# Second half's sums behind the first consumer matmuls, chunk masks built inside the first MLP, and a new order of ScalarE's work at the four norm boundaries

## The reference

```
for layer in range(2):
    a = rms_norm(h, norm_gains[layer, 0])
    m = mla_mixer(a, ...) if layer == 0 else hgrn2_mixer(a, ...)
    h = h + rms_norm(m, norm_gains[layer, 1])
    a = rms_norm(h, norm_gains[layer, 2])
    h = h + rms_norm(sq_relu_mlp(a, mlp_w1[layer], mlp_w2[layer]), norm_gains[layer, 3])
```

## Time and profile before

| | |
|---|---|
| runs shown | 1892.26, 1892.64, 1893.92 us; median 1892.64 us |
| profiled execution | 1893.63 us, span of its instructions 1891.7 us |
| mean granted TensorE clock | 0.947 |
| TensorE busy | 1697.2 us, 90% of the span |
| VectorE, ScalarE, GpSimd busy | 45%, 38%, 34% |
| HBM traffic | 73 GB/s over the span |

### The profile page before, as it was taken

One profiled execution on the slowest core, in us unless ns is written; L12 is line 12 of the kernel. 1 busy time (PEld: TensorE's weight loads), 2 busy tenths in 40 slices (PEclk: granted clock), 3 DMA queues, 4 the chain that ended last, 5 costly groups with the idle time before them and its releaser, 6 DMA issues.

```text
span 1891.7 us, 29823 instructions
## 1 busy us (share of the span) xinstructions
PE 1697.2 (90%) x10588; PEld 1374.1 (73%) x10588; DVE 853.8 (45%) x1467; ACT 716.4 (38%) x1129; POOL 635.0 (34%) x385
## 2 busy tenths in 40 slices
PE   4999968768678999899999997899998899999996
PEld 4778727755455676787888887788786787888885
DVE  4634377655566444352212124667664452212124
ACT  1332333322344443461323234666663452323231
POOL 4344500002331112444444445323232453444441
PEclk8999969998888999999999998899999999999997
DMA  9423200001211112323333332222221323333331
GB/s 313 133 78 92 75 11 3 4 2 48 55 37 29 34 36 61 90 68 94 95 90 99 99 93 75 56 56 74 59 78 34 89 78 89 94 95 100 89 100 56
DMA packets 250853, 140.10 MB, mean 74 GB/s; under 512 B 10089, under 2 KB 242624, under 8 KB 250768
## 3 DMA queue, kind: packets, MB, share of 16 engines
q1 hardware_dynamic: 249072, 135.03, 24.7%
q10 hardware_dynamic: 688, 2.23, 0.3%
q0 software_dynamic: 1008, 1.66, 0.3%
HBM read 136.80 MB, written 2.10 MB: 73 GB/s over the span
## 4 chain that ended last, share of the span: by engine, by line
issue 56%; POOL 15%; PE 15%; DVE 7%; DVEq 4%; ACT 1%; POOLq 1%; DMA 1%; ACTq 0%; SPq 0%
POOL w_low L510 13%; PE bank L661 6%; PE bank L805 2%; PE bank L916 2%; DVE bank L1770 1%; DVEq L1777 1%; DVEq L2139 1%; PE bank L819 1%; DVE mix_out L1770 1%; PE bank L1021 0%; DMA w_raw<-in_mlp_w 0%; POOL param_rows L491 0%; DVE kk_norm L1770 0%; DVEq L2075 0%; PE bank L788 0%
## 5 line engine op out<-in xcount | busy, mean ns | idle before, releaser
L510 POOL TENSOR_TENSOR w_low<-w_raw,w_high 128x1024 fp32r<-128x1024 f32 (+1 forms) x232 | 513.7, 2215 | 1124.9 <-ACT w_high L1293 1124.9
L661 PE MATMUL bank<-act_high,w_high 128*128 128x512 f32 x992 | 395.7, 399 | 13.9 <-POOL w_low L510 13.8
L661 PE MATMUL bank<-act_high,w_low 128*128 128x512 f32 x992 | 388.6, 392 | 0.0
L661 PE MATMUL bank<-act_low,w_high 128*128 128x512 f32 x992 | 388.3, 391 | 0.0
L1293 ACT ACTIVATE w_high<-w_raw 128x1024 fp32r<-128x1024 f32 (+1 forms) x232 | 225.2, 971 | 299.7 <-PE bank L661 273.9
L661 PEld LDWEIGHTS bank<-act_high,w_high 128*128 128x128 f32 x992 | 187.3, 189 | 61.1 <-issue 10.2
L661 PEld LDWEIGHTS bank<-act_high,w_low 128*128 128x128 f32 x992 | 187.0, 189 | 40.6
L661 PEld LDWEIGHTS bank<-act_low,w_high 128*128 128x128 f32 x992 | 187.5, 189 | 39.5 <-issue 2.0
L661 PE MATMUL bank<-hid_high,w_high 128*128 128x512 f32 x488 | 192.0, 394 | 3.9 <-DVE mix_out L2357 3.8
L661 PE MATMUL bank<-hid_low,w_high 128*128 128x512 f32 x488 | 191.3, 392 | 0.0
L661 PE MATMUL bank<-hid_high,w_low 128*128 128x512 f32 x488 | 191.0, 391 | 0.0
(11 more groups left out here) (509 smaller groups left out, 2893.4 us busy)
## 6 DMA issues: line engine op xcount, KB each, us to landing
w_raw<-in_mlp_w SPq DMA_DIRECT2D x128, 512.0 KB, 4.0
w_raw<-in_hgrn_w_in SPq DMA_DIRECT2D x32, 512.0 KB, 4.1
w_raw<-in_w_in SPq DMA_DIRECT2D x29, 512.0 KB, 3.9
w_ada_piece<-in_w_ada SPq DMA_DIRECT2D x6, 2048.0 KB, 13.5
w_raw<-in_w_out SPq DMA_DIRECT2D x8, 512.0 KB, 3.8
w_raw<-in_mla_w_o SPq DMA_DIRECT2D x8, 512.0 KB, 3.7
w_raw<-in_hgrn_w_o SPq DMA_DIRECT2D x8, 512.0 KB, 3.7
w_raw<-in_mla_w_in SPq DMA_DIRECT2D x6, 512.0 KB, 3.9
```

What stands on the lines that cost most here:

```text
L510: gp.tensor_tensor(WL[:, c0 % 2, 0:kt, 0:m], WR[:, c0 % 2, 0:kt, 0:m], WH[:, c0 % 2, 0:kt, 0:m].bitcast(F32), ALU.subtract).then_inc(w_lo, 1)
L661: mm = pe.matmul(PB[s][0:m, :], w[:, s, k, 0:m], a[:, k0 + k, :], start=(k == 0 and w is WH and a is hi), stop=(k == kt - 1 and w is WL))
```

## The change

`token_sum(b, 1)` leaves the last producer job. It and `token_stat(b, 1)` now hang on passes 0 and 3 of consumer job 1, and `token_spread(b, 1)` on pass 6 of job 0's `act_low` matmuls. At boundary 3 `token_sum` comes after four transposed tiles. GpSimd builds the chunk masks in four pieces between the splits F0+4 to F0+7 of the first MLP. On ScalarE, `high(c0+5)` and `high_x(c0+6)` go ahead of the square of tile 3, a one-element root is put ahead of the last square of half 0, and `high_x(c0+9)` behind that square.

```
-                             hooks={2: lambda: token_stat(b, 0, n_act)} if k == WHOLE else
-                             {6: lambda: token_sum(b, 1)} if k == KT - 1 else None).then_inc(job_done, 1)
+                             hooks={2: lambda: token_stat(b, 0, n_act)} if k == WHOLE else None)                        .then_inc(job_done, 1)
...
-                             hooks={4: lambda: token_spread(b, 1)} if i else
-                             {5: lambda: token_stat(b, 1, n_act + 3)})
+                             hooks={0: lambda: token_sum(b, 1), 3: lambda: token_stat(b, 1, n_act + 3)} if i else
+                             None)
                 for i in range(2):
-                    half_job(c1 + i, c0, head_bank(c1, i), 0, AH, AL, lo_pass, first=ready(act_lo, 0), last=AL)
+                    half_job(c1 + i, c0, head_bank(c1, i), 0, AH, AL, lo_pass, first=ready(act_lo, 0), last=AL,
+                             hooks=None if i else {6: lambda: token_spread(b, 1)})
...
             turn_out(0, 0, 4)
+            token_sum(3, 1)
             token_stat(3, 1, squares_at(3) + 3)
...
                 for k in range(WHOLE):
-                    if k or not prefetched:
+                    if k == 0 and not prefetched:
+                        high(c0 + 1)
+                    if 0 < k < WHOLE - 1:
                         high(c0 + 1 + k)
-                    if k == WHOLE - 1:
+                    if k == WHOLE - 2:
+                        high(c0 + WHOLE)
                         high_x(c0 + KT - 2, c0)
                     square_out(k, whole)
...
                 square_out(WHOLE + 1, HALF[0], PB[5])
+                act.activation(DEVC[:, 0:1], CST[:, 3:4], ACT.Sqrt)
+                square_out(WHOLE + 2, HALF[0])
                 if not last:
                     high_x(c0 + KT + 1, c0, done=c0 + WHOLE)
-                square_out(WHOLE + 2, HALF[0])
                 dev(0)
```

GpSimd's queue, with its four pieces (the masks' own instructions are those of L623 to L637 before):

```
             boundary(0, V0)
-            low_mlp(F0)
+            low(F0 + 4)
             gp.memset(TG[0][:, :], 1.0)
             gp.memset(HRST[:, :], 1.0)
+            gp.memset(AT[:, :, :], 0.0)
+            low(F0 + 5)
             gp.drain()
...
+            low(F0 + 6)
             gp.drain()
...
+            low(F0 + 7)
             gp.drain()
             gp.tensor_copy(HMSK[:, :, :].rearrange("p a t -> p (a t)"), TG[0][:, :])
-            gp.memset(AT[:, :, :], 0.0)
             gp.drain()
             gp.nop().then_inc(const_pool, 1)
+            low_mlp(F0, KT // 2)
+
             boundary(1, G0 - KT)
```

More of the change, by code:

```diff
@@ L611, in low_mixer_out, with low_mlp @@
                         low(c0 + s, i * 2)
-            def low_mlp(c0):
-                with gp.Fori(2, NQ * KT - 1) as i:
+            def low_mlp(c0, i0=2):
+                with gp.Fori(i0, NQ * KT - 1) as i:
                     for s in range(2):
```

## The result

The changed kernel takes 1880.48 us (median of 4 runs, 1878.75 to 1881.90) against 1893.10 us for the kernel before on the same chip (1892.26 to 1893.92): a ratio of 0.9932, 95% interval 0.9916 to 0.9948. The profiled execution took 1878.75 us, the fastest of the four and the only one of them inside that range, with a span of 1876.9 and a mean granted clock of 0.952.

The account below looks back on a forecast made before the run. TensorE, busy 1697.2 of 1891.7 us, was taken as the bound, with 29 us of waits in reach. Boundary gains of 4.7, 6.3, 4.1 and 3.6 us sum to 18.7, said as 19: median 1873.6 us, range 1866.5 to 1879.5.

Parts of the forecast that it names:

- Scalar engine order: ScalarE at the norm boundaries: earlier `high`, `low` and root make the first half's chain 2.45 us earlier at boundary 0.
- Masks: GpSimd at boundary 1: removes the 3.62 us wait for `w_low_x` and 1.5 us of slow clock; hidden in MLP 0.
- Second half's sums: Norm boundaries: `token_sum` moved behind consumer work lets the eviction go at once; residual earlier by 0.75 or 2.8 us.
- the slow end: From the second half's sums to its residual at the 1.2 GHz clock: 6.15 us, against 4.1 at full clock.
- The 13 matmuls: TensorE's spread stands 13 matmuls later in the queue, leaving 105 behind it instead of 118: 1.5 us less.
- MLP entries: ScalarE's eight squares for the next norm may run late at the MLPs' entry: taken as 0, at worst 0.5 us each.
- norm_sum: Boundary 1: its 2.55 us wait for VectorE's sums of squares grows to about 4 us.
- first sign: Prediction is wrong if the residual of the second half does not move by 3 us or more.
- the wait only moves: Rival: the reordered chain is late elsewhere, such as `high_x(c0+9)` on its DMA; gain 13.7 us, 1878.9 us; chance 0.15.
- Full clock: Rival: TensorE keeps full clock through the consumer jobs; gain 25 us, 1867.4 us; chance 0.2.
- The slower case: Rival: the clock, once fallen in the scattered stretch, stays down behind the sums; 1940 us; chance 0.03.

Follow-up runs that it names:

- e7: The changed kernel with GpSimd's `low_x(c0+9)` in two instructions of half the size; 1880.75 us in one execution.
- e4: The changed kernel with the root of half 0 put ahead of `high_x(c0+9)`; 1881.64 us, 0.9942 of the kernel before.
- e6: The changed kernel with the edits of e4 and e5 together; 1870.35 us, 0.9878 of the kernel before.
- e8: e4 without extra matmuls, the first two consumer jobs side by side, pass by pass; 1872.17 us, 0.9888 of the kernel before.
- e12: The changed kernel measured once more, unedited; 1882.04 us, 0.9937 of the kernel before.
- e5: The changed kernel with four extra unread matmuls behind each of passes 3 to 6 of the first consumer job; 1879.08 us, 0.9929 of the kernel before.
- e10: e6 with ScalarE's eight squares for the next norm moved behind the MLP's second and third `high`; 1870.63 us, 0.9882 of the kernel before.
- e9: e6 with one extra matmul in each gap instead of four; 1870.51 us, 0.9891 of the kernel before.

## Why the prediction was off, step by step

**The step that failed** is "Scalar engine order" (at boundary 1 together with "Masks"), which made the first half's chain earlier by 2.45, 5.5, 2.0 and 1.25 us, 11.2 in all; it is 4.31. ScalarE's side came for the most part: the reciprocal is earlier by 1.94, 4.43, 1.60 and 0.55 us, 8.5 in all. From there to the diagonals the forecast counted "as before". They are held for 1.69, 1.41, 1.12 (boundary 2 was already touched before, 1.05 for 0.48) and 0 us, and 1.94 - 1.69, 4.43 - 1.41, 1.60 - 1.12 and 0.55 are, to 0.01, the 0.26, 3.01, 0.49 and 0.55 measured. The forecast asked when each instruction may start and took its length from the row; the length itself depends on what runs beside it on GpSimd. The root and `high_x(c0+9)` changed places in time, so GpSimd's instruction, 0.1 us behind `high_x`, and VectorE's, 0.4 behind the root, now meet. (The terms for boundary 0 did not add up as written, either: 1.05 + 0.75 + 1.28 - 0.4 is 2.68, not 2.45.)

The Trainium skill states this (SBUF — State Buffer, "Who interferes with whom"): VectorE and GpSimd share a pair of ports to SBUF as an exclusive lock that the one that starts first keeps for its whole instruction, and on VectorE's side instructions with two SBUF inputs take part, and `tensor_scalar` can. The rows here agree, with e7's most of all: 2.17 for 0.48 us, 1.57 for 0.16, and each of these small instructions that was held ended within 0.1 us of the GpSimd instruction that it met. The prediction did not weigh this rule.

The other 2.7 us of that step (11.2 less 4.3 and 4.2 of holds) were lost ahead of the reciprocal, and smaller meetings of the same kind stand there. TensorE still waits for `w_low_z` 0.79 at boundaries 1 to 3, where 0.3 was forecast: at boundary 1 `low_z` takes 2.87 us for 2.38, starting 0.06 us behind VectorE's 128x512 add:

```profile
1139.56 0.69 DVE L1779 TENSOR_TENSOR sum_sq<-tmp,sum_sq 128x512 f32<-128x512 f32 x1 [0.22 <-issue]
1139.62 2.87 POOL L525 TENSOR_TENSOR w_low_z<-w_raw,w_high_z 128x1024 fp32r<-128x1024 f32 x1 [1.84 <-ACT w_high_z L1565]
```

At boundary 0 it is the add that is held, 2.80 us for 0.69, and the sum waits 0.28. Which is held depends on tenths of a microsecond; that these meetings make up all of the 2.7 is argued, not shown.

**Was it the hold?** Only in part, and this the experiments had to show. e4 takes the hold away and the time stays: what it wins at the sums, 4.9 us, comes back behind them with a longer stretch at half clock. What caps this kernel behind the sums is the pair: while TensorE's clock falls there, earlier sums meet slower matmuls. So the forecast of 19 us would not have been met without the hold either. Why the clock was down for longer once the sums came earlier is open; that it was the clock is shown by e6 and e8, which keep it up and keep the gain.

**Second half's sums: right in mechanism, with luck in the size.** 7.36 us for 4.5 in the profile of the result, which had the clock on its side; in that of e12, the same kernel, the sums to the residual are 3.8 us shorter than before, with 7.00 and 6.57 us beyond the slow end of 6.15. I took the slow end at 6.15 us; it came at 5.68 and 5.67 with the clock down, and at 4.35 at boundary 1, where it stayed up (4.1 forecast for that). Both values that I held apart were nearly there, and which one applies was the right question, but the answer changes with boundary and execution. The 13 matmuls brought 1.50 and 1.49 for 1.5. At boundary 3, 2.12 for 2.35.

The rule of the Trainium skill (TensorE: Matmul & The Clock Gate, "The HAM clock gate") that the prediction cited agrees with these traces: with pairs of matmuls the clock fell in two of three heads of the changed kernel and in all three in e12; with more matmuls in each gap, read (e8) or not (e5), the granted clock was 1.00 from there to the residual in all three.

**Masks: right on where they hide, right in sum only with the order.** No split in the MLP waits for them. **MLP entries:** taken at 0, at worst 0.5; measured 0.51, twice, and e10 shows ScalarE's squares as their cause. **`norm_sum`:** 4.01 us for "about 4".

**Its own signs.** By its first sign the forecast was wrong: the residual of the second half should have moved by 3 us or more, and measured from the start of the half jobs it moved by 1.48 at boundary 0, 1.67 at boundary 2 and 2.67 at boundary 3 (5.85 at boundary 1). `w_low_z` stayed at 0.79 for "under 0.3", too.

**The rivals.** The number lies nearest to "the wait only moves" (1878.9, 1.6 us below it), which gave the first half's gain away. It named `high_x(c0+9)` late on its DMA; it starts without a wait (781.82), so the place was right in effect and not in mechanism. "Full clock" (1867.4) needs both causes gone, and then it nearly holds: 1870.35. The slower case showed in no profile: behind the sums the clock always came back inside the head.

## What to carry to other kernels

When an edit moves small VectorE work in time, look at what GpSimd runs then: a 0.2 us instruction on the critical path was held here for the rest of a 2.4 us one, and the cure of the hold was one line, the short chain first and the long prefetch behind it. Where TensorE has to wait for pieces, try to give each piece more matmuls (two jobs abreast) rather than the fewest; here thinly filled gaps cost up to 3 us a head in slow clock (7.21 us from the sums to the residual in e4, 4.14 in e6). And try causes in pairs before dropping one: two edits that bring 0 and 1.4 us alone brought 10 together. Lastly, one profile against another can mislead by some 3 us here, because the clock falls at other places from execution to execution.

## What the runs showed of the hardware that I had not expected

- A 128x2 multiply on VectorE took 1.57 us for 0.16 when it met a GpSimd subtract of 2.37 us; two pieces of 1.29 and 1.26 us held two successive VectorE instructions to the end of one piece each.
- It goes the other way too: `low_z`, started while VectorE added, took 2.87 us for 2.38.
- One more matmul in each of four gaps, about 0.9 us apart, went with a granted clock of 1.00 in all three heads of e9's profiled execution. Four more executions took the same time at the same mean clock; the sixth took 9 to 10 us longer at 0.949.
- The stretch at half clock was 3.4 us at boundary 0 in one execution of the changed kernel and 6.8 in another. Stretches of 3.4 us also stood inside the MLPs of some executions and not of others.
